# Page gathers that wait for score bursts, and cache copies moved into the second feed-forward block, in a two-layer hybrid decoder step

## The chip, the cores and the metric

One Trainium2 chip, one NeuronCore of it. The metric is the device time of one execution in microseconds (us), the median of several. A core has TensorE (PE; its weight loads are PEld), VectorE (DVE), ScalarE (ACT), GpSimd (POOL), SyncE (SP, which here only issues transfers), and 16 DMA engines that all queues share.

## What is computed

One inference step of a two-layer decoder for 256 prompt tokens and 8 samples of 8 tokens with 2048 past positions each, in float32. Each layer is a feed-forward block, token mixing, and a second feed-forward block:

```python
x += 0.5 * post1(SwiGLU_1(pre1(x)))
h  = pre_mix(x); proj = h @ w_in          # columns for branches A, B, C and gates
#   A: RWKV-7 time mixing;  B: dilated window attention;  C: latent attention
m = sum_b gate_b * (y_b @ w_branch_b);  x += post_mix(m @ w_out)
x += 0.5 * post2(SwiGLU_2(pre2(x)))
```

Branch C for a sample attends over 16 pages of a paged cache, found through a page table:

```python
ckv=cache_mla_ckv[l][page_table]          # 8 samples x 2048 rows x 256
s = (einsum('bqhc,blc->bhql', ql, ckv_all) + einsum('bqhr,blr->bhql', qr, krope_all)) * scale
return einsum('bhql,blc->bqhc', softmax(masked(s)), ckv_all)
```

Besides the result, the step returns the new states. Among them are the windows of keys and values of branch B for each sample: the old window without its first 8 rows, followed by the new ones. So 2040 of 2048 rows are copied from input to output, for 8 samples, keys and values, both layers.

## The kernel before

All engines run their own instruction streams, written out by hand, and meet on counting semaphores. `S[name]` counts steps, and `wait_ge(S[name], n)` waits until n of them are done.

**The samples' latent attention** (`ml_sample`, on TensorE, VectorE and ScalarE). For sample b, TensorE runs a burst of 144 matmuls of 32 rows by 64 columns on 256 keys (`scores`, which counts `ml_mm` at its end), then small pieces (`by_channel`, `own_tokens`), the value product of the sample before (`values(b - 1)`, 34 matmuls, counts `ml_pv`), and the transposes of the shares (`shares(b, r)`), the last of which takes the own tokens' share from VectorE. VectorE turns gathered keys into the layout that `scores` needs (`keys`: the low half of sample b+1 first in the round, before the maximum of sample b; the high half after it), takes the maximum over PSUM, and writes the own share (`own_share`). ScalarE takes the exponential.

**Page gathers** (GpSimd, from line 682). For each sample three indirect transfers of 2.25 MB together (one of the rotated keys, two of the latent rows, L698 and L701) go into one of four buffers. Before, those of samples 2 and 3 wait for the prompt's attention, those of samples 4 to 7 for `ml_pv` of b - 3, that is for the value product that last read the buffer. In time, this is just ahead of the burst of sample b - 2.

**Window copies** (GpSimd, `copied`, L674). 16 copies of 4080 KB, from DRAM to DRAM, in each layer, each waiting for the one before. `COPY_AT = (3, 11)`: three run from the input projection on, eight during the RWKV stage, and the last five right behind the last gather, that is during the last samples' attention and the output projection.

**Feed-forward weights** (SyncE, L646). A ring of three slots. A unit of the first half is 1 MB of gate and 1 MB of up weights (`f2 gu u`, 11 units), loaded when the unit three before it has been used; for unit 3 that is `ffn_gu` reaching 4, the end of unit 0. VectorE makes sums of quarters of unit u+1 during unit u (`weight_sums`, L2096 to L2102, a Strassen-like scheme), and TensorE waits for the second of these sums in unit u+1. The third branch's weights (`br c`) are loaded when `ml_pv` reaches 5.

The functions around the change, with the line numbers of the profile:

Of the kernel before, what the change touches and what calls it, by code (L numbers as in the profile page):

```python
# [141 lines left out]
GU0, SG0, TOK0 = {"f1": 0, "f2": 2}, {"f1": 0, "f2": 12}, {"f1": 0, "f2": 17}  # L142
# [137 lines left out]
def build(nc, io):  # L280
    SCB, SCC = DH ** -0.5, (DNOPE + DROPE) ** -0.5
    with ExitStack() as ctx:
# [3 lines left out]
        def sem(name):  # L286
            return ctx.enter_context(nc.semaphore(name))
# [33 lines left out]
        def cut(buf, at, a, b, rows=P):  # L321
# [85 lines left out]
        kr_at = [(big, 3072, big, 5120, big, 7168), (reg, 10720, reg, 12768, reg, 14816), (ring, 0, ring, 2048, ring, 4096),  # L407
                 (ring, 9088, h_flat, 0, h_flat, 2048)]
        KRc = [[cut(b0, at0, 8, KV_LORA), cut(b1, at1, 8, KV_LORA)] for b0, at0, b1, at1, _, _ in kr_at]
        KRr = [buf[:, at:at + 512] for _, _, _, _, buf, at in kr_at]  # L410
        QL = reg[:, 2016:15328].rearrange("p (c n) -> p c n", c=2)
        KTl = [cut(ring, 4608 + 2048 * i, 4, 512) for i in range(2)]
# [21 lines left out]
        S = {n: sem(n) for n in STEPS}  # L434
# [5 lines left out]
        units = weight_units(io)  # L440
        slot_of, before = weight_slots(units)
        uidx = {name: i for i, (name, _) in enumerate(units)}

        heads = [("f1", "gu", u) for u in range(HEAD)]
# [39 lines left out]
        def layer_begun(eng, l):  # L484
            eng.sem_inc(s_arrive, 1)
            eng.wait_ge(s_go, l + 1)
            eng.sem_inc(s_pad, 1)

        def lay(ap, l):
            return ap[bass.ds(l, 1)]  # L490
# [166 lines left out]
        @block.gpsimd  # L657
        def _(pool):
            for i in range(8):
                pool.dma_start(ptab[N_PAGES * i:N_PAGES * i + N_PAGES, :], io["page_table"].rearrange("b n -> n b"), allow_slow_non_contiguous=True).then_inc(s_copy, 16)  # L660
            pool.wait_ge(s_copy, TABLE)
            for l in range(DEPTH):
                layer_begun(pool, l)

                def copied(first, last):
                    for i in range(first, last):
                        if i:

                            pool.wait_ge(s_copy, l * (16 * 2 * NB) + TABLE + 16 * i)
                            pool.sem_inc(s_pad, 1)  # L670
                        b, n = i // 2, "kv"[i % 2]
                        src = lay(io["cache_swa_" + n], l)[:, b, TS:PAST].rearrange("a r n -> (a r n)")
                        dst = lay(io[f"o_swa_{n}_s"], l)[:, b, 0:PAST - TS].rearrange("a r n -> (a r n)")
                        pool.dma_start(dst.rearrange("(q n) -> q n", q=240),  # L674
                                       src.rearrange("(q n) -> q n", q=240)).then_inc(s_copy, 16)

                pool.wait_ge(S["pam"], 1)
                copied(0, COPY_AT[0])
                pool.wait_ge(S["streams"], 1)
                copied(COPY_AT[0], COPY_AT[1])  # L680
                pool.wait_ge(S["pages_ready"], 1)
                for b in range(NB):
                    if b == 0:
                        pool.wait_ge(S["sws_done"], NB)
                    elif b == 1:
                        pool.wait_ge(S["prompt_mm"], 2 * H + 16)
                        pool.wait_ge(S["ml_prep"], 1)
                    elif b in (2, 3):

                        pool.wait_ge(S["prompt_y"], 2 * H)  # L690
                        pool.wait_ge(S["ml_prep"], 1)
                        pool.wait_ge(S["pgm"], 24)
                    else:

                        pool.wait_ge(S["ml_pv"], b - 3)
                    rows_of = lambda i: bass.IndirectOffsetOnAxis(ap=pidx[:, i * NB + b:i * NB + b + 1], axis=0)
                    src = io["cache_mla_krope"].rearrange("l n (s r) c -> (l n s) (r c)", s=8)
                    pool.indirect_dma_start(out=KRr[b % 4], out_offset=None, in_=src, in_offset=rows_of(0)).then_inc(s_kr[b % 4], 16)  # L698
                    src = io["cache_mla_ckv"].rearrange("l n (s r) c -> (l n s) (r c)", s=16)
                    for half in range(2):  # L700
                        pool.indirect_dma_start(out=KRc[b % 4][half].rearrange("p n c -> p (n c)"), out_offset=None, in_=src, in_offset=rows_of(1 + half)).then_inc(s_kr[b % 4], 16)  # L701
                copied(COPY_AT[1], 2 * NB)
                pool.wait_ge(s_copy, l * (16 * 2 * NB) + TABLE + 16 * 2 * NB)

# [2133 lines left out]
```

## Time and profile before

| | |
|---|---|
| median of 3 runs | 2613.18 us (2611.27 to 2618.77) |
| profiled execution | 2636.64 us, its span 2634.8 us |
| granted TensorE clock, mean | 0.99 |
| TensorE busy | 2542.8 us (97%) |
| VectorE busy | 1314.5 us (50%) |
| ScalarE busy | 560.7 us (21%) |
| DMA moved | 505.66 MB, mean 192 GB/s |

The page gives one profiled execution on a time axis that starts at its span. "Idle before, releaser" tells how long an engine stood still ahead of an instruction and what ended that; "issue" means that nothing the profile shows did. PEclk is the clock granted to TensorE, 1.00 being 2.4 GHz and 0.50 1.2 GHz. The first layer ends near 1320 us; the second repeats its pattern some 1303 us later.

### The profile page before, as it was taken

Reading aid. Unit: us, or ns where it says so; the run is one execution under the profiler, and the core shown is the slowest. Engines: PE = TensorE matmul, PEld = TensorE weight load, DVE = VectorE, ACT = ScalarE, POOL = GpSimd, SP = SyncE. Lnnn points to the kernel's source line nnn. Section 1 sums busy time; section 2 is a strip of 40 time slices with the busy share of each in tenths; the row PEclk is TensorE's granted clock in tenths of the full one; section 3 lists DMA queues with packets and bytes.
Section 4 is the critical chain, followed back from the end, with each engine's and each line's share of the span. In section 5 each row is a group of like instructions: output and inputs, shape, how many; then the busy total and the mean of one; then the engine's idle time right before and its main releaser. Section 6 shows DMA issues by size and latency. Waiting matters only on the chain.

```text
span 2634.8 us, 52961 instructions
## 1 busy us (share of the span) xinstructions
PE 2542.8 (97%) x23108; PEld 2063.0 (78%) x23108; DVE 1314.5 (50%) x2847; ACT 560.7 (21%) x1249; POOL 67.4 (3%) x92
## 2 busy tenths in 40 slices
PE   7999999999999999999999999999989999999998
PEld 6999856655666667999999997566556666689998
DVE  4663553335543372665376535533455334627654
ACT  2110231133422221301021112311334222221010
POOL 0000000000000110000000000000000001100000
PEclk9999999999999899999999999999999998999999
DMA  6434679632962469544544456684439433794443
GB/s 228 145 114 143 225 241 335 225 122 117 383 262 71 157 214 373 162 132 118 144 146 131 120 175 248 226 321 177 173 134 395 181 120 137 272 333 147 131 111 86
DMA packets 260549, 505.66 MB, mean 192 GB/s; under 512 B 9760, under 2 KB 198560, under 8 KB 245216
## 3 DMA queue, kind: packets, MB, share of 16 engines
q1 hardware_dynamic: 251616, 330.83, 38.0%
q0 software_dynamic: 8704, 171.45, 17.6%
q8 instruction: 183, 3.00, 0.5%
q14 instruction: 46, 0.38, 0.0%
HBM read 491.95 MB, written 140.85 MB: 240 GB/s over the span
## 4 chain that ended last, share of the span: by engine, by line
PE 89%; DVE 5%; ACT 2%; DMA 2%; issue 1%; PEld 0%; SPq 0%; DVEq 0%
PE ps L716 84%; PE ps L719 6%; DMA big<-in_cache_swa_k_dram 1%; DMA ring<-in_f_wu_dram 1%; PEld ps L716 0%; ACT big L1841 0%; DVE reg L2009 0%; ACT reg L1841 0%; DVE ring L2507 0%; DVE x L2001 0%; DVE reg L2290 0%; SPq L580 0%; DVE reg L2584 0%; ACT reg L1712 0%; DVE ring L2522 0%
## 5 line engine op out<-in xcount | busy, mean ns | idle before, releaser
L716 PE MATMUL ps<-reg 128*128 128x160 f32 (+12 forms) x4584 | 513.2, 292 | 2.5 <-issue 1.6
L716 PEld LDWEIGHTS ps<-reg 128*128 128x128 f32 (+5 forms) x4584 | 453.7, 163 | 34.5 <-issue 25.1
L716 PE MATMUL ps<-h,ring 128*128 128x320 f32 (+2 forms) x1984 | 449.0, 378 | 17.4 <-DMA ring<-in_f_wu_dram 13.5
L716 PE MATMUL ps<-reg,ring 128*128 128x160 f32 (+1 forms) x3040 | 458.9, 306 | 0.0
L716 PEld LDWEIGHTS ps<-reg,ring 128*128 128x128 f32 x3040 | 426.1, 189 | 16.4 <-issue 6.2
L716 PEld LDWEIGHTS ps<-h,ring 128*128 128x128 f32 (+1 forms) x1984 | 323.0, 189 | 108.4 <-issue 28.5
L716 PE MATMUL ps<-ring,h 128*128 128x512 f32 (+3 forms) x896 | 246.6, 469 | 0.0
L716 PE MATMUL ps<-big,ring 128*128 128x160 f32 (+2 forms) x2016 | 214.6, 279 | 7.6 <-DVE big L2427 4.5
L716 PEld LDWEIGHTS ps<-big,ring 128*128 128x128 f32 (+2 forms) x2016 | 197.7, 168 | 28.2 <-issue 17.3
L716 PEld LDWEIGHTS ps<-ring,h 128*128 128x128 f32 (+1 forms) x896 | 103.1, 163 | 78.8 <-issue 62.9
L716 PE MATMUL ps<-big,reg 32*64 32x256 f32 (+8 forms) x2144 | 144.9, 363 | 3.3 <-issue 3.2
L716 PEld LDWEIGHTS ps<-big,reg 32*64 32x64 f32 (+4 forms) x2144 | 107.4, 139 | 30.9 <-issue 22.9
L719 PE MATMUL ps<-cst,big 128*128 128x128 f32 (+1 forms) x672 | 98.3, 283 | 18.4 <-ACT big L1841 7.3
L719 PEld LDWEIGHTS ps<-cst,big 128*128 128x128 f32 (+1 forms) x672 | 72.2, 140 | 38.9 <-ACT big L1841 12.4
L716 PE MATMUL ps<-ring,reg 32*64 32x256 f32 (+2 forms) x1312 | 90.3, 403 | 4.8 <-issue 3.4
L716 PE MATMUL ps<-ys,ring 128*128 128x320 f32 x256 | 79.0, 454 | 8.9 <-DVE reg L2555 8.9
L716 PE MATMUL ps<-ring 128*16 128x128 f32 (+3 forms) x1888 | 86.1, 261 | 0.0
L1687 ACT ACTIVATE reg<-ps 128x320 f32<-128x320 f32 x40 | 17.5, 439 | 316.8 <-PE ps L716 316.8
L719 PE MATMUL ps<-cst,reg 128*128 128x128 f32 (+3 forms) x436 | 73.5, 288 | 11.0 <-ACT ring L1895 6.0
L716 PEld LDWEIGHTS ps<-ring 128*16 128x16 f32 (+3 forms) x1888 | 69.8, 111 | 14.6 <-issue 13.6
L716 PEld LDWEIGHTS ps<-ring,reg 32*64 32x64 f32 (+1 forms) x1312 | 49.5, 140 | 38.7 <-issue 26.6
L719 PEld LDWEIGHTS ps<-cst,reg 128*128 128x128 f32 (+3 forms) x436 | 50.3, 143 | 33.4 <-issue 16.2
(320 smaller groups left out, 2642.3 us busy)
## 6 DMA issues: line engine op xcount, KB each, us to landing
out_o_swa_k_s_dram<-in_cache_swa_k_dram POOLq DMA_DIRECT2D x16, 4080.0 KB, 15.3
out_o_swa_v_s_dram<-in_cache_swa_v_dram POOLq DMA_DIRECT2D x16, 4080.0 KB, 16.5
ring<-in_w_in_dram SPq DMA_DIRECT2D x30, 2048.0 KB, 8.9
ring<-in_f_wd_dram SPq DMA_DIRECT2D x32, 1408.0 KB, 7.0
ring<-in_f_wg_dram SPq DMA_DIRECT2D x42, 1024.0 KB, 5.5
ring<-in_f_wu_dram SPq DMA_DIRECT2D x42, 1024.0 KB, 8.1
big<-in_cache_swa_k_dram SPq DMA_DIRECT2D x32, 1024.0 KB, 8.2
ring<-in_cache_swa_v_dram SPq DMA_DIRECT2D x32, 1024.0 KB, 7.2
```

The costliest lines, as they stand in the source:

```text
L716: return pe.matmul(out, lhsT, rhs, start=first, stop=last, skip_group_check=True)
L719: return pe.transpose(out, in_, ident[0:rows, 0:rows])
L1687: act.activation(GU[u % 2][:, :, 0, 0:HT], summed(X), ACT.Copy).then_inc(S["gu_act"], 1)
```

## The change

GpSimd gets three more waits. The gathers of samples 2 and 3 also wait for the first score burst (`ml_mm` 1), those of samples 4 to 7 for the burst of sample b - 2, counted from zero (`ml_mm` b - 1). The last five copies of the layer wait until unit 0 of the second feed-forward block is done (`ffn_gu` 4, the same point that releases the load of its unit 3). Nothing else is changed; in particular the transfers are the same.

```diff
                         pool.wait_ge(S["prompt_y"], 2 * H)
                         pool.wait_ge(S["ml_prep"], 1)
                         pool.wait_ge(S["pgm"], 24)
+                        pool.wait_ge(S["ml_mm"], 1)
                     else:
 
                         pool.wait_ge(S["ml_pv"], b - 3)
+                        pool.wait_ge(S["ml_mm"], b - 1)
                     rows_of = lambda i: bass.IndirectOffsetOnAxis(ap=pidx[:, i * NB + b:i * NB + b + 1], axis=0)
...
                         pool.indirect_dma_start(out=KRc[b % 4][half].rearrange("p n c -> p (n c)"), out_offset=None, in_=src, in_offset=rows_of(1 + half)).then_inc(s_kr[b % 4], 16)
+                pool.wait_ge(S["ffn_gu"], GU0["f2"] + 2)
                 copied(COPY_AT[1], 2 * NB)
```

## Rows read from the trace of the kernel before

**Rows 1.** The page, busy time, share of the span, instructions
```profile
PE 2542.8 (97%) x23108; PEld 2063.0 (78%) x23108; DVE 1314.5 (50%) x2847; ACT 560.7 (21%) x1249; POOL 67.4 (3%) x92
```

**Rows 2.** Windows over score bursts and both layers' loops; the last three: clock, DMA, GB/s
```profile
899.28:911.40 12.12, 10.70 (x148) 5.72 (x147) 0.31 (x2) 0.00 (x0) 5.37 (x6) 0.72 0.85 314
917.16:923.11 5.95, 5.95 (x146) 3.88 (x145) 5.18 (x11) 0.70 (x2) 0.00 (x0) 0.67 0.02 4
929.02:935.21 6.19, 5.37 (x146) 3.90 (x145) 2.91 (x8) 0.79 (x3) 1.95 (x3) 1.00 0.77 258
...
979.70:983.77 4.07, 4.07 (x145) 3.25 (x144) 2.56 (x8) 0.80 (x3) 0.00 (x0) 1.00 1.28 428
...
899.28:996.74 97.46, 88.93 (x1486) 59.63 (x1484) 60.50 (x139) 21.79 (x55) 17.75 (x20) 0.93 0.64 233
2202.47:2298.75 96.28, 89.72 (x1484) 59.68 (x1483) 60.49 (x139) 21.80 (x55) 17.71 (x20) 0.93 0.64 233
```

**Rows 3.** Timeline of TensorE: start, duration, what, idle before and its releaser
```profile
915.01 1.97 PE L719 MATMUL ps<-cst,reg 128*128 128x128 f32 x8 [3.01 <-ACT ring L1895]
...
932.38 0.53 PE L716 MATMUL ps<-ring,reg 32*64 32x256 f32 x6 [0.77 <-issue]
...
941.53 0.24 PE L719 MATMUL ps<-cst,ring 64*64 64x64 f32 x1
```

**Rows 4.** Timeline of GpSimd: gathers of samples 2 and 4, first and last of five copies
```profile
899.01 0.95 POOL L698 DMA_INDIRECT ring<-in_cache_mla_krope_dram,pidx  x1 [12.57 <-PE ps L716]
...
928.16 0.94 POOL L698 DMA_INDIRECT big<-in_cache_mla_krope_dram,pidx  x1 [21.98 <-PE ps L716]
...
969.64 0.55 POOL L674 DMA_DIRECT2D out_o_swa_v_s_dram<-in_cache_swa_v_dram  x1
...
1042.92 0.50 POOL L674 DMA_DIRECT2D out_o_swa_v_s_dram<-in_cache_swa_v_dram  x1 [16.85 <-DMA out_o_swa_k_s_dram<-in_cache_swa_k_dram]
```

**Rows 5.** Windows of 1 us at the ends of two gathers' data
```profile
914.00:915.00 1.00, 0.00 (x0) 0.00 (x0) 1.00 (x2) 0.96 (x4) 0.00 (x0) 0.61 0.08 33
...
937.00:938.00 1.00, 1.00 (x12) 0.68 (x10) 0.88 (x5) 0.72 (x1) 0.00 (x0) 1.00 0.14 57
```

**Rows 6.** Timeline of VectorE in the third sample's round: maximum, own share, key transposes
```profile
935.32 1.23 DVE L2705 TENSOR_REDUCE sml<-ps 128x1 f32<-128x1024 f32 x1 [3.18 <-PE ps L716]
...
940.71 0.15 DVE L2717 COPY ring<-ring 64x8 f32<-64x8 f32 x1
...
940.89 2.37 DVE L2650 STREAM_TRANSPOSE ring<-big 128x1024 f32<-128x1024 f32 x2
```

**Rows 7.** Timelines in the second feed-forward block: SyncE, VectorE (unit 3, 4), TensorE
```profile
1084.71 0.37 SPq L646 DMA_DIRECT2D ring<-in_f_wg_dram  x1
...
1109.38 1.22 DVE L2096 TENSOR_TENSOR reg<-ring 128x1024 f32<-128x1024 f32 x1
...
1124.59 1.22 DVE L2096 TENSOR_TENSOR reg<-ring 128x1024 f32<-128x1024 f32 x1
...
1117.12 2.34 PE L716 MATMUL ps<-reg 128*128 128x160 f32 x16
```

**Rows 8.** Time to landing, loads issued at 996.9, 1021.7, 2298.9, 2323.7, 1085.1
```profile
ring<-in_w_out_dram SPq DMA_DIRECT2D x1, 2048.0 KB, 28.6
...
ring<-in_f_wu_dram SPq DMA_DIRECT2D x1, 1024.0 KB, 38.1
...
ring<-in_w_out_dram SPq DMA_DIRECT2D x1, 2048.0 KB, 15.9
...
ring<-in_f_wu_dram SPq DMA_DIRECT2D x1, 1024.0 KB, 37.4
...
ring<-in_f_wu_dram SPq DMA_DIRECT2D x1, 1024.0 KB, 9.0
```

**Rows 9.** DMA queues from 1042.9 to 1060: packets, MB, share of 16 engines
```profile
q0 software_dynamic: 80, 4.18, 65.9%
q1 hardware_dynamic: 1805, 1.82, 33.5%
```

## The prediction

> **What bounds the kernel now.** I read the page first, then TensorE's waits, then the sample part of latent attention by windows, and last what the DMA engines do beside it. TensorE is busy for 97% of the span [rows 1], so only what stretches or idles TensorE counts. The place that the change touches is the loop over the eight samples, 97.5 us in the first layer and 96.3 us in the second [rows 2]. Each sample has one burst of 144 small score matmuls. With no gather in flight the seventh burst takes 4.07 us; the third takes 6.19 us and the first 12.12 us, both beside gathers; the second, with idle DMA, takes 5.95 us at a granted clock of 0.67 [rows 2]. The bursts of samples 4 to 6 are like the third (6.16 to 6.19 us). Inside the third, TensorE stands still for 0.77 us with "issue" as the only reason [rows 3]. These holes come 2 to 4 us after GpSimd starts issuing a gather [rows 4] and are over by about 1.2 us after its last issue, though the data flies on until 937. What starves is therefore the supply of instructions to a very dense burst, at the start of a gather, and not the data.
>
> **Part one: the gathers wait for the bursts.** The gather for sample b (4 to 7) now starts at the end of burst b-1 instead of at the end of the value product before it. It then runs beside the value product, whose matmuls are about a quarter as dense, and should be out of its starving phase before the next burst, 6.5 us later (the burst of the third sample ends at 935.2, the next begins at 941.7). In itself that is 6.17 - 4.07 = 2.1 us for each of four bursts. But the gather starts later, and a new wait may end last. Its flight is 9.3 us from first issue (928.2) to last data (about 937.5) [rows 4, 5]. Then VectorE turns the keys (2.37 us) and makes a divisor before it may take the next maximum, with some eight small instructions another 1.2 us: 3.6 us in all. From the maximum to the end of the own share 5.5 us pass (935.32 to 940.86) [rows 6], and TensorE needs that share at 941.53, 6.3 us after the burst's end at 935.2 [rows 3]; the slack is 0.8 us. So burst b+1 ends no earlier than 0.3 + 9.3 + 3.6 + 5.5 + 0.2 + 4.1 = 23.0 us after burst b-1, where two undisturbed periods would be 2 x 10.6 = 21.2 us and two of now are 25.3 us. Over bursts 4 to 8 this gives about 56.5 us against 61.5 us in the first layer (935.2 to 996.7), where copies also cost the last two samples some 1.5 us, and 59.9 us in the second.
>
> One collision is new. The load of the third branch's weights (2 MB) starts after the fifth value product; that comes 5 us into the flight of the last gather, where before the gather had landed. Two transfers share the engines for some 2.5 us, so I charge 2 us in each layer. Gains here: 3 us and 1.5 us.
>
> The first two bursts: the gathers for samples 2 and 3 (six issues in some 7 us from 899.0 on, data until about 914) [rows 4, 5] move from the first burst's start to its end. The first burst should then take 4.1 us, a gain of 8.1 us. The wait of 3.0 us for the exponential behind it stays [rows 3], and with it the fall of the clock to half. The second burst now meets the end of the six issues: I take the 3 us that it overlaps as nearly lost (some 15 of 144 matmuls, the density of the first burst at 904 to 907), and the rest partly at full clock, since the low clock now covers less of it. That comes to 7 us against 5.95 us. Keys for sample 2 are in by 13.8 us after the stretch's start, 3.6 us before the second maximum wants them: it comes at most 0.5 us late. The stretch up to the third burst's end goes from 35.9 to about 26.8 us, a gain of 9.1 us (9.5 us in the second layer). **Sum of part one: 12.1 + 11.0 = 23 us**, bounds 14 and 31 us: the low end has a half clock through the whole second burst (3 us a layer) and 0.4 us of holes in each value product; the high end has gathers that are fast enough for the undisturbed period.
>
> **Part two: the last five copies move.** They leave the end of the attention and the output projection, where TensorE never waits for weights, and start when the first unit of the second feed-forward block is done, at 1084.7, together with the load of unit 3 [rows 7]. GpSimd's queue has nothing behind them until the next layer, so the wait for f2 itself costs nothing. The loads are what counts. That block takes one unit of 2.1 MB per 15.2 us. Unit 3's sums begin at 1109.38 and unit 4's at 1124.59 [rows 7], with loads issued at 1084.7 and 1097.75. TensorE takes the second sum at 1117.12, 3.5 us of VectorE work after the landing, so unit 3 may land up to 28.9 us after 1084.7, and the following ones up to 44.1, 59.3 and 74.5 us. Without copies such a load lands in 9.0 us [rows 8].
>
> Beside copies it doesn't. The five copies stand 17 to 21 us apart (969.6 to 1042.9) [rows 4]. In the stretch of the last of them, with weights waiting all through it, the weights' queue (q1) moved 1.82 MB in 1805 packets in 17.1 us, the copy's (q0) 4.18 MB in 80 [rows 9]; the block wants 2.36 MB in that time. Counted from the copy issued at 990.8, the first 2.1 MB asked for after it landed at 34.6 us (996.9 + 28.6) and the third 2.1 MB at 69.0 us (1021.7 + 38.1); in the second layer the first landed at 21.3 us (2298.9 + 15.9, copy at 2293.5), the third at 67.6 us [rows 8]. Against the limits of 28.9 and 59.3 us the third unit is late by 8.3 to 9.7 us in both layers, and the fourth, one copy period of 17.2 us on, by some 10 to 13. Lateness here isn't added up: each wait moves the later limits. So a layer loses the largest, **11.5 us, 23 us in both**, bounds 0 and 27 us. Zero is possible, since copies and loads start together and the average rate (0.12 MB per us over the two last copies) falls short by only 2.3 us a unit, which the slack of 9.7 us would just cover if landings weren't lumpy. I take the landings, since they are the same thing measured twice. A fall of the clock in such a wait costs up to 3 us in each layer and is in the upper bound.
>
> The trace's rows show why: weights come in lumps between copies. The Trainium skill, "DMA: Bandwidth & Descriptors", section "Queues, rings and completion order", says that a DMA engine alternates between the queues that have work, a whole packet at a time. That speaks against this change, since a copy's packets are long and the weights' rows short, and the trace agrees. By the page the loss would be that of the landings, by the average rate next to nothing.
>
> **The sum.** The profiled execution took 2636.6 us (its span 2634.8), 0.9% over the median of 2613.2 us; both terms are differences in microseconds and carry over. 2613.2 - 23 + 23 = **2613 us**. The gain of the samples is given back in the feed-forward block. For this likeliest case alone the range is 2604 to 2622 us.
>
> **The rivals.** (1) The copies are hidden in the feed-forward block: part one is kept, 2613 - 23 = 2590 us, 2582 to 2600 with its bounds. For it: the average rate, and a slack of two units; the second layer's first load fitted between two copies (21.3 us). Against it: both third loads. (2) Slower: the weights of the second feed-forward block, starved by copies, are late by the full 13.5 us with the clock falling in the waits, 2 x 15 = +30 us, while the sample loop gives only 14 us: 2629 us. It decides from the point where the loss of a layer exceeds 11.5 us. For it: two idle times of 3 us are each followed by half clock in the sample loop. (3) The holes aren't the gather's: the bursts keep their length wherever the gather stands, part one gives nothing and the gathers only come later, 2613 + 23 = 2636 us. Against it: the seventh burst, 4.07 us, in both layers. The Trainium skill, "Runtime: NRT & Kernel Launch", section "Instruction fetch mechanics", calls the crossing of an instruction block "mostly hidden"; by that rule part one would give nothing but the clock. The holes of 0.77 us speak against it.
>
> **Chances.** Forecast 0.52, (1) 0.28, (2) 0.14, (3) 0.06. Some 0.3% (8 us) is what a measurement of this kernel can tell from no change. Faster: (1) and 0.05 of the forecast's edge, 0.33; slower: (2), (3) and 0.02, 0.22; the same: 0.45. The range takes in most of (1) and of (2): 2588 to 2630 us.
>
> **What would show it.** First burst near 4.1 us, third to sixth near 4.1 us without issue holes, the period alternating between 10.6 and 12.4 us: part one. VectorE waiting on a gather's landing ahead of its key transposes: the 9.3 us are the bound. In the second feed-forward block: VectorE and TensorE waiting for weight landings of units 3 to 6, landings of 20 to 38 us instead of 9, and a block longer by some 11 us. If no such wait is there, part two is wrong and rival (1) holds. If the holes appear in the value products instead, part one only moved them.

## The result, and the profile after

The changed kernel took 2650.1 us (median of 4 runs, 2632.8 to 2654.6) against 2613.9 us before (4 runs, 2611.3 to 2618.8): a ratio of 1.013, interval 1.010 to 1.0159. The kernel got 36 us slower. The forecast was 2613 us in a range of 2588 to 2630, so the measured time lies 37 us above the forecast and 20 us above the range. The ratios in this document are given with their 95% interval as they were recorded; they are not the quotients of the two medians and lie up to 0.13% away from them, so differences of 0.1% are not read.

The profile's page of the kernel after, as [rows 1]: busy time, then the chain of work that ended last by engine, then the group of matmuls that waits most for weights.

```profile
PE 2535.9 (96%) x23108; PEld 2063.9 (78%) x23108; DVE 1313.9 (50%) x2847; ACT 559.0 (21%) x1249; POOL 67.4 (3%) x92
...
PE 85%; DVE 5%; DMA 4%; ACT 2%; issue 2%; PEld 0%; SPq 0%; POOL 0%; DVEq 0%; POOLq 0%
...
L719 PE MATMUL ps<-reg,ring 128*128 128x160 f32 (+1 forms) x3040 | 460.7, 306 | 11.4 <-DMA ring<-in_f_wu_dram 11.4
```

TensorE is busy for 7 us less than in [rows 1], and yet the profiled span is longer, 2652.8 us against 2634.8: what came are waits. Windows over the first six score bursts and the two loops, as [rows 2] (PE busy, PEld, DVE, ACT, POOL, then granted clock, DMA share, GB/s):

```profile
901.96:906.09 4.13, 4.13 (x148) 3.75 (x146) 0.31 (x2) 0.00 (x0) 0.00 (x0) 1.00 0.01 4
911.05:916.76 5.71, 5.71 (x145) 3.81 (x144) 2.77 (x3) 0.70 (x2) 2.53 (x3) 0.70 1.00 374
927.25:933.39 6.14, 6.14 (x145) 4.00 (x144) 2.98 (x8) 0.70 (x2) 0.00 (x0) 0.65 0.02 7
939.89:943.96 4.07, 4.07 (x146) 3.24 (x145) 0.00 (x0) 0.79 (x3) 0.00 (x0) 1.00 0.81 328
953.78:957.86 4.08, 4.08 (x146) 3.25 (x145) 3.07 (x7) 0.70 (x2) 0.00 (x0) 1.00 0.02 6
964.35:970.92 6.57, 4.71 (x146) 3.38 (x145) 2.15 (x2) 0.79 (x3) 0.00 (x0) 1.00 0.51 197
901.96:996.37 94.41, 80.97 (x1485) 57.09 (x1483) 60.09 (x139) 21.41 (x55) 16.95 (x18) 0.93 0.49 174
2219.10:2313.21 94.11, 80.95 (x1486) 56.99 (x1484) 60.36 (x139) 21.43 (x55) 16.94 (x18) 0.91 0.48 175
```

The first burst is whole, 4.13 us, as forecast. But the loops are only 3.1 and 2.2 us shorter than in [rows 2], not 12 and 11 us. (That pair turns out to be of two kinds of execution; the like for like comparison stands further down.) The reader sees where it went in VectorE's timeline, with GpSimd's of the gathers that it waits for:

```profile
907.01 0.95 POOL L700 DMA_INDIRECT ring<-in_cache_mla_krope_dram,pidx  x1 [17.90 <-PE ps L719]
...
934.33 0.95 POOL L700 DMA_INDIRECT big<-in_cache_mla_krope_dram,pidx  x1 [20.14 <-PE ps L719]
...
918.12 2.37 DVE L2653 STREAM_TRANSPOSE ring<-ring 128x1024 f32<-128x1024 f32 x2 [4.30 <-DMA ring<-in_cache_mla_ckv_dram,pidx]
...
921.62 1.21 DVE L2708 TENSOR_REDUCE sml<-ps 128x1 f32<-128x1024 f32 x1
...
944.53 2.37 DVE L2653 STREAM_TRANSPOSE ring<-big 128x1024 f32<-128x1024 f32 x2 [5.40 <-issue]
```

and in TensorE's:

```profile
925.11 1.97 PE L722 MATMUL ps<-cst,reg 128*128 128x128 f32 x8 [3.56 <-ACT ring L1898]
...
951.52 1.09 PE L722 MATMUL ps<-cst,reg 128*128 128x128 f32 x8 [1.27 <-ACT ring L1898]
953.61 0.24 PE L722 MATMUL ps<-cst,ring 64*64 64x64 f32 x1 [1.00 <-DVE ring L2720]
...
970.33 0.65 PE L719 MATMUL ps<-big 32*64 32x256 f32 x6 [1.86 <-issue]
...
972.04 5.36 PE L719 MATMUL ps<-big,reg 128*64 128x256 f32 x32
...
1170.56 4.04 PE L719 MATMUL ps<-reg,ring 128*128 128x160 f32 x16 [10.18 <-DMA ring<-in_f_wu_dram]
```

VectorE stands ahead of the key transposes until a gather has landed: 11.1 us after its first issue for sample 2 (907.01 to 918.12), 10.2 us for sample 4 (934.33 to 944.53). For sample 2 the view names the transfer. For sample 4 it says "issue", and the reading rests on the DMA share, which is 0.28 from 943 to 944 and 0.00 from 944 to 945. The maximum, due at 916.9 when the second burst ends, is taken at 921.62; TensorE idles 3.56 us, the clock falls, and the third burst runs for 6.14 us at a granted clock of 0.65. The last line is in the second feed-forward block: one unit's weights are 10 us late, and their issue on SyncE's queue itself took 23 us, where it takes 0.58 us in the trace of before:

```profile
1143.44 23.43 SPq L646 DMA_DIRECT2D ring<-in_f_wu_dram  x1
```

Two profiles 18 us apart don't explain medians 36 us apart, and the profiled execution of before was 23 us above the median of the timed runs of the same kernel. What lay in that 23 us is what the experiments had to find.

### The profile page after: what moved, and what is told of

It is laid out like the page before. It is cut to its first block, busy times and chain, and to the rows that moved or that the text cites. A ratio compares the mean times of both kernels' runs of the same rounds, so it can differ in the third digit from the quotient of the medians.

```text
span 2652.8 us, 52973 instructions
## 1 busy us (share of the span) xinstructions
PE 2535.9 (96%) x23108; PEld 2063.9 (78%) x23108; DVE 1313.9 (50%) x2847; ACT 559.0 (21%) x1249; POOL 67.4 (3%) x92
## 4 chain that ended last, share of the span: by engine, by line
PE 85%; DVE 5%; DMA 4%; ACT 2%; issue 2%; PEld 0%; SPq 0%; POOL 0%; DVEq 0%; POOLq 0%
PE ps L719 79%; PE ps L722 6%; DMA ring<-in_f_wu_dram 3%; DMA ring<-in_cache_mla_ckv_dram,pidx 1%; ACT big L1844 1%; PEld ps L719 0%; ACT reg L1844 0%; DVE reg L2012 0%; DMA reg<-in_cache_mla_ckv_dram,pidx 0%; DMA h<-in_cache_mla_ckv_dram,pidx 0%; DVE ring L2510 0%; DVE ring L2653 0%; DVE x L2004 0%; DVE reg L2293 0%; DVE big L2653 0%
## 5 line engine op out<-in xcount | busy, mean ns | idle before, releaser
L719 PE MATMUL ps<-reg,ring 128*128 128x160 f32 (+1 forms) x3040 | 460.7, 306 | 11.4 <-DMA ring<-in_f_wu_dram 11.4
L719 PEld LDWEIGHTS ps<-ring,h 128*128 128x128 f32 (+1 forms) x896 | 103.8, 165 | 80.1 <-issue 64.3
L719 PE MATMUL ps<-big,reg 32*64 32x256 f32 (+8 forms) x2144 | 136.2, 359 | 0.2 <-issue 0.2
L1690 ACT ACTIVATE reg<-ps 128x320 f32<-128x320 f32 x40 | 17.5, 437 | 308.6 <-PE ps L719 308.6
L719 PE MATMUL ps<-ring,reg 32*64 32x256 f32 (+2 forms) x1312 | 78.3, 433 | 0.0
L1693 ACT ACTIVATE ys<-reg 128x640 f32<-128x640 f32 x40 | 29.5, 737 | 209.1 <-DVE reg L2243 209.1
## 6 DMA issues: line engine op xcount, KB each, us to landing
out_o_swa_v_s_dram<-in_cache_swa_v_dram POOLq DMA_DIRECT2D x16, 4080.0 KB, 16.8
```

The lines of the kernel that those rows point to most:

```text
L719: return pe.matmul(out, lhsT, rhs, start=first, stop=last, skip_group_check=True)
L1690: act.activation(GU[u % 2][:, :, 0, 0:HT], summed(X), ACT.Copy).then_inc(S["gu_act"], 1)
L1693: act.activation(SG[u % 2], GU[u % 2][:, 0], ACT.Sigmoid).then_inc(S["ffn_sg"], 1)
```

## The experiments

The runs were made in five groups. All ratios are to the kernel before, timed in the same group on the same chip.

**First group: the parts alone.** Both gather waits, copies at their old place; the copies alone; and the waits of samples 4 to 7 alone. Each leaves the other added lines out (cut):

```diff
 # gathers_only, both lines; late_gathers_only, the second alone
+                        pool.wait_ge(S["ml_mm"], 1)
+                        pool.wait_ge(S["ml_mm"], b - 1)
 # copies_only
+                pool.wait_ge(S["ffn_gu"], GU0["f2"] + 2)
```

> Part one alone: the gathers of samples 2 to 7 wait for the bursts, the last five copies stay behind the last gather. Theory A (the loss sits in the second feed-forward block, the sample loop gains a little): 2609 us, 0.1 to 0.4% under before, the stretch of a layer's eight bursts some 94 us instead of 97. Theory B (the gathers' new waits cost more than the bursts gain): over before by 0.5% or more, 2627 us and up, with waits of VectorE on gather landings ahead of its key transposes.

Measured: 2642.4 us against 2643.5, ratio 0.9992 (0.9976 to 1.0008). That is neither of the two theories and not a gain of 23 us: no difference shows.

> Only the gathers of samples 4 to 7 wait for a burst; those of samples 2 and 3 start as before, and the copies stay. Against part one whole it tells what the wait of the first two costs: theory A' (moving them idles TensorE ahead of the third burst and keeps its clock low, so they are worth only the 8 us of the first burst less some 8 us): within 3 us of part one whole. Theory B': they carry the gain, and this kernel is 5 us or more slower than part one whole.

Measured: 2650.7 us, 1.0023 (1.0007 to 1.004): this half costs 6 to 7 us. An issue hole (idle time that the profile ends with "issue" alone) of 2.68 us stands in its last burst.

> Part two alone: the gathers start where they did, the last five copies start after unit 0 of the second feed-forward block. Theory A: the whole loss is here, 2640 to 2650 us (+1.0 to 1.4%), with one or more waits of TensorE on weights landing in the second feed-forward block of each layer. Theory B: within 0.4% of before.

Measured: 2648.4 us, 1.0022 (1.0003 to 1.0041): 5 us lost, not 23.

The fourth kernel is the changed one with the last five copies of a layer each cut into two DMAs of alternate 2 KB rows (only the main lines are shown; the semaphore counts change with them):

```diff
+                        if i >= COPY_AT[1]:
+                            src = lay(io["cache_swa_" + n], l)[:, b, TS:PAST].rearrange("a (r e) n -> (a r) e n", e=2)
+                            dst = lay(io[f"o_swa_{n}_s"], l)[:, b, 0:PAST - TS].rearrange("a (r e) n -> (a r) e n", e=2)
+                            for e in range(2):
+                                pool.dma_start(dst[:, e], src[:, e]).then_inc(s_copy, 16)
+                            continue
```

> The changed kernel, with each of the last five copies of a layer split into its even and its odd rows of 2 KB, so that its packets are about as short as the weights'. Theory of the packets (a DMA engine takes turns between queues by packet, so long copy packets hold up the weights): the waits for weights in the second feed-forward block vanish, 10 us or more faster than the changed kernel, 2610 to 2640 us. Rival (the engines' total rate is the bound, 0.38 MB per us for both): waits and time as in the changed kernel, 2650 us.

Measured: 2630.6 us, 0.9955 (0.9938 to 0.9973), the first version below before. The copies' DMA queue and the weight loads from 1080 to 1170 us, first in the changed kernel (`changed_once_more`, below) and then in this one (packets, MB, share of 16 engines; for the loads KB each and median us to landing):

```profile
q0 software_dynamic: 398, 20.89, 62.1%
...
ring<-in_f_wg_dram SPq DMA_DIRECT2D x6, 1024.0 KB, 24.0
ring<-in_f_wu_dram SPq DMA_DIRECT2D x6, 1024.0 KB, 25.5
```

```profile
q0 software_dynamic: 4332, 17.15, 56.0%
...
ring<-in_f_wg_dram SPq DMA_DIRECT2D x7, 1024.0 KB, 12.1
ring<-in_f_wu_dram SPq DMA_DIRECT2D x6, 1024.0 KB, 16.8
```

The copies go in eleven times as many packets for 18% fewer bytes in that stretch, and the weights land in 12.1 and 16.8 us instead of 24.0 and 25.5; TensorE waits for no weight in that block, in either layer. The chip doesn't explain it: `copies_only`, timed beside this kernel, has 23.7 and 25.4 us. So the length of the copies' packets made the weights late. In exchange the copies themselves move more slowly when cut: 17.15 MB against 20.89 MB in the 90 us, while the weights' queue moves 12.58 MB against 9.22. The Trainium skill, "DMA: Bandwidth & Descriptors", section "Queues, rings and completion order", has an engine alternate between queues by whole packets; this pair of rows agrees.

**Second group: again, and the copies taken apart.**

> The changed kernel on the same footing as the partial ones. By the sum of the two parts measured alone (-1 us and +5 us) it is 2 to 6 us over before, ratio 1.000 to 1.003. If the two parts hinder each other, or if the first measurement holds wherever it is run, it is 1.3% (30 us or more) over before.

Measured: 2642.4 us against 2645.4, ratio 1.0001 (0.9981 to 1.0021). The 1.3% was gone, with the kernel unaltered. In its trace TensorE waits 2.6 us for weights in the first layer's block where the trace of after waits 10.2.

The next two have the gathers of before; the copies are cut as above, and stand in the second feed-forward block or at their old place. The third leaves the last five copies of each layer out (two outputs stay incomplete).

> The gathers as before; the last five copies in the second feed-forward block, split into rows of 2 KB. If short packets alone bring the gain: 2630 us, 13 us under before. If it needs the gathers' new waits too: within 3 us of before less the 5 us that the long-packet copies cost there, about 2640 us.

Measured: 2638.5 us, 0.9978 (0.9959 to 0.9998).

> The kernel before with nothing changed but the packets of the last five copies of a layer (rows of 2 KB). If long packets of the copies also hold up the fetch of TensorE's instructions in the last bursts: 2 to 8 us under before, without issue holes in the seventh and eighth burst. If only the place counts: as before.

Measured: 2642.3 us, 0.9992 (0.9972 to 1.0012): inconclusive.

> The kernel before without the last five copies of each layer (that part of the window copies is left out). It tells what copies at the old place cost: by the trace of before some 1.5 us of issue holes in the first layer and 0.2 us in the second, so 0 to 4 us under before. If it is 10 us or more under before, the copies cost more at their old place than the trace's holes show, and moving them has that much to win.

Measured: 2636.0 us, 0.9969 (0.9952 to 0.9986). These copies cost about 8 to 9 us where they were (4 to 13 us by the interval), in stages for which the prediction had charged them 1.5 us.

**Third group: is before itself the same each time?** Two kernels unaltered, the changed one without the last copies, and the changed one with all sixteen copies cut.

```diff
 # late_gathers_no_last_copies, on the changed kernel
-                pool.wait_ge(S["ffn_gu"], GU0["f2"] + 2)
-                copied(COPY_AT[1], 2 * NB)
 # all_copies_in_2kb_rows, on copies_in_2kb_rows
-                        if i >= COPY_AT[1]:
+                        if True:
```

> The kernel before, unaltered, as a run of its own. It tells what the ruler is worth. The first comparison had before at 2613.9 us and the changed kernel at 2650.1 us; on two later chips before stood at 2643.5 and 2645.4 us and the changed kernel at 2642.4 us. Theory: the absolute time of before depends on the chip, and the two are equal on each of them; then this run has a ratio of 1.000 +- 0.002, and its absolute time is again in 2640 to 2648 us. Rival: before has executions near 2613 us that the changed kernel lacks; then some of these twelve are under 2625 us.

Measured: 2613.0 us against 2613.9, ratio 0.9997 (0.9984 to 1.0011). Within the group before repeats itself, and the level is not the 2644 us of the first two groups.

> The changed kernel, unaltered, beside before on a further call. Theory (the changes cancel): ratio 0.998 to 1.003, some 2642 us if before is at 2644 us. Rival (the first comparison, 1.3% slower, is what the change does): ratio above 1.008, 2665 us.

Measured: 2647.1 us, 1.0126 (1.0109 to 1.0143). The 1.3% was back. So the changed kernel took 2642 to 2650 us in all three comparisons, and before is what moves, between 2613 and 2644. Windows over the first three bursts and over both loops in the trace of `before_again`, to be laid beside [rows 2]:

```profile
899.44:903.58 4.14, 4.14 (x148) 3.75 (x146) 0.31 (x2) 0.00 (x0) 3.23 (x4) 1.00 0.54 135
908.54:914.30 5.76, 5.76 (x146) 4.29 (x145) 5.62 (x9) 0.70 (x2) 0.00 (x0) 0.70 0.93 382
920.21:924.28 4.07, 4.07 (x146) 3.24 (x145) 3.10 (x8) 0.79 (x3) 1.97 (x3) 1.00 0.66 197
...
899.44:979.55 80.11, 75.25 (x1486) 55.21 (x1484) 60.35 (x139) 21.78 (x55) 17.78 (x20) 0.98 0.74 271
2192.71:2273.80 81.09, 76.86 (x1486) 55.47 (x1484) 60.45 (x139) 21.79 (x55) 17.75 (x20) 0.96 0.74 272
```

The same program, the same gather issued 0.3 us ahead of the first burst (899.17), and the burst takes 4.14 us, not 12.12. The third takes 4.07 us beside its gather (DMA share 0.66). The loops take 80.1 and 81.1 us against 97.5 and 96.3: 32.5 us in both. One microsecond of each burst, in the profile that I had and in `before_again`:

```profile
901.00:902.00 1.00, 0.93 (x9) 0.44 (x12) 0.00 (x0) 0.00 (x0) 0.69 (x2) 1.00 0.76 229
```

```profile
901.00:902.00 1.00, 1.00 (x49) 1.00 (x41) 0.00 (x0) 0.00 (x0) 0.69 (x2) 1.00 0.66 217
```

The gather moves as much (229 and 217 GB/s) at the same full clock, and TensorE starts 9 matmuls or 49. A gather beside a burst is not enough to stretch it. I call the two kinds of execution stretched and whole.

> The changed kernel with the last five copies of each layer left out (two outputs stay unwritten for the last samples). The same left out of the kernel before gave 2636.0 us against 2645.4 us, a ratio of 0.9969. So this run against that one is the worth of the late gathers with no copies about. Theory (the gathers' holes are traded against waits for their landing and half-clock bursts): within 3 us of 2636 us at a before of 2645 us, ratio 0.995 to 0.998. Rival (my first sum: part one is worth 23 us): 2613 us, ratio 0.988.

Measured: 2637.1 us, 1.0087 (1.007 to 1.0104) against a whole before (four runs). The late gathers alone cost over 23 us there; the copies in the feed-forward block add 10 us (2647.1 - 2637.1).

> The changed kernel with all sixteen copies of a layer, not only the last five, split into two DMAs of 2 KB rows each. With the last five split it took 2630.6 us against 2643.5 us, a ratio of 0.9955. Theory (long packets make weight loads late only where the load has little slack, which is the second feed-forward block): the first eleven copies lie beside projections and prompts that don't wait for weights, so nothing more is gained; ratio 0.994 to 0.997. Rival (long packets cost wherever copies run): another 5 us or more, ratio under 0.993. Doubled issues on GpSimd could also cost: then above 0.998.

Measured: 2626.5 us, 1.0052 (1.0035 to 1.007), 20.6 us below the changed kernel of its group. That is more than leaving the last copies out gives, so the rival holds: the first eleven copies' long packets cost too, over 10 us, and where exactly isn't settled (no single wait that went stands out in their stages).

**Fourth group: a trace of a stretched before beside its time, and the halves.** `only_samples_2_and_3_wait` has of the change only the first added wait; the two others are kernels of above.

> The kernel before, unaltered, with a trace. Theory (stretched bursts are the whole difference between before at 2613 us and before at 2644 us): if its median is above 2635 us, its first score burst takes some 12 us and the bursts of samples 2 and 4 to 6 some 6.2 us, 11 to 13 us a layer; if it is under 2620 us, all bursts but the second take some 4.1 us. Rival (the level differs for another reason, all over the span): a slow one with whole bursts, or a fast one with stretched bursts.

Measured: 2640.2 us against 2644.8 (0.9988, 0.9972 to 1.0003). Windows over the fourth burst and over both loops:

```profile
944.48:950.74 6.26, 5.74 (x146) 3.78 (x145) 2.59 (x8) 0.80 (x3) 1.98 (x3) 1.00 0.79 267
901.76:998.95 97.19, 88.83 (x1486) 59.86 (x1484) 60.52 (x139) 21.79 (x55) 17.78 (x20) 0.93 0.64 233
2209.53:2306.10 96.57, 88.28 (x1486) 59.80 (x1484) 60.52 (x139) 21.79 (x55) 17.79 (x20) 0.93 0.64 234
```

Stretched, with a time at the upper level: its loops are 32.6 us longer than those of `before_again` (97.2 + 96.6 against 80.1 + 81.1), its profiled execution 32.3 us (2643.95 against 2611.63). In this pair the stretched loops are the whole difference of level. The profile that the prediction was made from differs from `before_again` by 32.5 us of loops too, but by only 25.0 us in all: between the two loops it is 7.4 us shorter, in stages that are the same program. Single executions vary by that much elsewhere.

> The second part alone: the last five copies in the second feed-forward block, gathers as before. On a chip where before took 2643.5 us it cost 4.8 us (ratio 1.0022). Theory: the loss is one of weight landings and has nothing to do with the bursts, so it is the same on any chip: 3 to 9 us more than before, ratio 1.001 to 1.0035. Rival (the second part costs more where the bursts are whole): ratio above 1.005.

Measured: 2642.9 us, 0.9988 (0.9975 to 1.0001). With the 1.0022 of the first group: between -2 and +5 us, for a part that I had at +23.

> Half of the first part: the gathers of samples 2 and 3 wait for the first score burst, those of samples 4 to 7 start as before, copies as before. Waiting of samples 4 to 7 alone gave 1.0023, both waits 0.9992, on a chip with stretched bursts. Theory: there this half is the good one, since it mends the 12 us burst and costs one landing wait: ratio 0.994 to 0.998. On a chip with whole bursts it only brings the landing wait and the half-clock burst behind it, some 6 us a layer: ratio 1.003 to 1.006. Rival (the waits of the first part are what costs everywhere): above 1.000 on either.

Measured: 2629.6 us, 0.9956 (0.9931 to 0.9982), on a stretched before; five runs only, from 2619.3 to 2641.1. This is the good half, as expected, though VectorE waits 4.71 us for sample 2's gather in its trace.

> Gathers as before, last five copies in the second feed-forward block and split into two DMAs of 2 KB rows. It gave 0.9978 on a chip where before took 2645.4 us. Theory: short packets take the loss of the second part away and keep the copies from the end of the attention, on any chip: ratio 0.996 to 0.9995. Rival: on a chip where before takes 2613 us nothing is to be had from the copies: ratio 1.000 to 1.003.

Measured: 2636.7 us, 0.9965 (0.995 to 0.998).

**Fifth group: the landing wait, priced.** Old gathers but for sample 3, or samples 2 and 3; last copies cut and in the second feed-forward block.

```diff
 # samples_2_and_3_wait_2kb: without the condition
+                        if b == 3:
+                            pool.wait_ge(S["ml_mm"], 1)
```

> Only the gathers of samples 2 and 3 wait for the first score burst; last five copies in the second feed-forward block as 2 KB rows. The two halves gave 0.9956 and 0.9965 to 0.9978 alone. Theory (their gains lie in different stages and add): 0.992 to 0.995 where before takes some 2644 us (2623 to 2631 us); where before takes 2614 us, the landing wait of sample 2 and the half-clock third burst cost 5 us a layer and the copies give 4 to 8: 1.000 to 1.004. Rival: they don't add, 0.996 or more, or 1.006 or more on a chip with whole bursts.

> As the other kernel of this call, but only sample 3's gather waits for the first burst; sample 2's starts beside it as in the kernel before. Theory (the landing of sample 2's gather is what this half costs): no idle time for it ahead of the third burst's round, on any chip. Where bursts are stretched, three issues remain beside the first burst, which then takes 6 to 8 us instead of 12, the third burst has full clock, and the total is that of the other kernel within 3 us. Where bursts are whole: 3 to 10 us below the other kernel, at or just below before, ratio 0.997 to 1.000. Rival (any gather beside the first burst, ahead of the exponential's wait, costs the whole stretch): first burst 10 us or more on a chip with stretched bursts, 8 us or more above the other kernel.

The record gives the same chip number for this group and the first one, and before now took 2616.0 us, not 2643.5. So the expectations above, which put whole and stretched down to the chip, are wrong in that: one chip showed both, and in the fifth group the fourth and fifth bursts, beside unchanged gathers, took 4.07 us in both traces. Measured: 2618.9 us, 1.0012 (0.9998 to 1.0026), with both samples waiting; 2607.6 us, 0.9967 (0.9953 to 0.9982), with sample 3 alone. Loops of the one and of the other:

```profile
897.54:980.98 83.44, 76.83 (x1486) 55.14 (x1484) 60.45 (x139) 21.67 (x55) 16.94 (x18) 0.96 0.55 197
2193.84:2279.10 85.26, 79.46 (x1486) 56.42 (x1484) 60.53 (x139) 21.66 (x55) 16.93 (x18) 0.92 0.54 193
```

```profile
906.89:985.90 79.01, 75.39 (x1486) 54.41 (x1484) 60.33 (x139) 21.77 (x55) 16.64 (x18) 0.98 0.57 208
2200.15:2278.88 78.73, 75.46 (x1486) 54.93 (x1484) 60.33 (x139) 21.78 (x55) 16.65 (x18) 0.98 0.58 209
```

11.0 us of loop, 11.3 us of median, and all of the 11.0 lies ahead of the third burst's end (29.5 against 24.8 us from the loop's start in the first layer, 32.0 against 25.7 in the second). The two kernels differ only in the wait of sample 2's gather, so its late landing is the price of moving it: in the first layer a 3.26 us wait of TensorE, the next 2.14 us at a granted clock of 0.50 and a third burst of 4.54 us, in the second layer a third burst of 7.66 us at 0.62. In the kernel where sample 3 alone waits the third bursts took 4.07 and 4.89 us. (The two profiled executions are only 0.2 us apart, since that of the second kernel spent 9.4 us more ahead of the loop, where the kernels are the same; it is the slowest of its six runs.) The second version is the only one that beat a whole before, by 0.3% (0.9967, 0.9953 to 0.9982); it was not run against a stretched one.

## Why the prediction was wrong

**The step that failed** is the sentence that the profiled execution lay 0.9% over the median and "both terms are differences in microseconds and carry over". They were not of the same thing. The profile was of a stretched execution (its loops of 97.5 and 96.3 us are like the 97.2 and 96.6 of `before_on_another_chip`); that the median of 2613.2 us was of whole ones is read from its level, that of `before_again`. The 23.4 us between them were not noise around a common kernel; part one's gain of 23 us was the mending of what those runs did not have. From the whole kernel's 80.1 and 81.1 us the changed loops of 93.9 us are 26.6 us longer:

```profile
901.10:995.03 93.93, 80.80 (x1486) 57.91 (x1484) 60.40 (x139) 21.42 (x55) 16.92 (x18) 0.93 0.48 175
2212.04:2305.95 93.91, 81.72 (x1486) 57.25 (x1484) 60.27 (x139) 21.47 (x55) 16.95 (x18) 0.91 0.48 175
```

Those two rows are of `changed_once_more`. Its waits for weights in the second feed-forward block are 3.8 us in the first layer (2.2 + 1.6 below) and 3.5 in the second; 26.6 + 7.3 = 33.9 us of the 36.5 us between its profiled execution and that of `before_again`. The remaining 2.6 us are not traced; stages that the change doesn't touch vary by more than that.

```profile
PE ps L719 <- DVE reg L2103: 2.2, 2, 1.2
PE ps L719 <- DMA ring<-in_f_wu_dram: 1.6, 1, 1.6
```

**Part one against a stretched before** is a term of the sum that was mis-sized. The fair pair for it is a changed kernel in a group where before is stretched. Both loops of `changed_again`, and its second burst:

```profile
903.21:994.12 90.91, 78.88 (x1486) 56.03 (x1484) 60.27 (x139) 21.44 (x55) 17.00 (x18) 0.96 0.50 181
2207.77:2299.30 91.53, 80.62 (x1486) 57.25 (x1484) 60.45 (x139) 21.44 (x55) 16.98 (x18) 0.93 0.49 180
912.32:919.24 6.92, 6.58 (x145) 4.17 (x144) 2.99 (x4) 0.70 (x2) 2.53 (x3) 0.78 0.98 376
```

Against [rows 2] that is 6.5 and 4.8 us of loop, 11.3 us in both, where 12.1 and 11.0 were forecast; the low bound was 14. The first burst took 4.14 us (forecast 4.1) and the second 6.92 (forecast 7). The gather of sample 2, with the three issues of sample 3 behind it, took 10.75 us from its first issue to the key transposes, not 9.3. TensorE idled 1.93 and 0.67 us ahead of the third burst, whose end came 28.8 us after the stretch's start, not 26.8. From there to the eighth burst's end it took 62.1 us, where 56.5 us and 2 us for a collision were forecast and 61.5 us stand in the trace of before: this is the larger part of the miss.

The trace of after, of the group with a whole before, shows the same steps at a higher price. Its second burst took 5.71 us and was done at 14.8 us from the stretch's start; the keys, forecast "in by 13.8 us" with the maximum "at most 0.5 us late", were in at 16.2 us (918.12 - 901.96), and the maximum came 4.7 us late. The idle time of 3.56 us dropped the clock on the third burst (+2.1 us), which the forecast had charged nowhere; its end came 31.4 us after the stretch's start. From the third burst's end to the fifth's, forecast at 23.0 us, 24.5 us passed (933.39 to 957.86): 0.94 us from the burst's end to the issue instead of 0.3, 10.2 us to the transposes instead of 9.3. From the fourth's end to the sixth's it was 27.0 us and from the fifth's to the seventh's 25.3 us, with new starvation, as the forecast's last sentence allowed: a hole of 1.86 us in the sixth burst and a value product of 5.36 us for 3.67.

The value product starts just behind the gather issued at 971.78; the value product at 946.01, as close behind one, takes its 3.67 us, so why this one is long isn't settled. The hole is tied to a place in the program and not to that gather. Nine of the traces have an issue hole at this very place in the first layer, with six matmuls of the burst left, among them `changed_again`, `samples_2_and_3_wait_2kb` and `only_sample_3_waits_2kb`, and none of the three traces of before has one:

```profile
968.71 0.65 PE L719 MATMUL ps<-big 32*64 32x256 f32 x6 [1.67 <-issue]
959.02 0.66 PE L727 MATMUL ps<-big 32*64 32x256 f32 x6 [0.26 <-issue]
```

In all nine a packet of the instruction queue (q8 in the profile) starts 0.4 to 2.2 us ahead of the hole. That the hole waits for it is likely and not shown.

**Part two**: mechanism right, size wrong. Landings went from 9.0 us [rows 8] to some 24 us, inside the 20 to 38 forecast, and VectorE and TensorE waited for weights as forecast, though later in the block (from 1138 to 1181 us). But the waits cost TensorE 7.3 us in `changed_once_more`, 10.2 us for one unit in the profile of after, and -2 to +5 us net in the two runs of the copies alone, not 23. One thing was left out: the copies had a price at the old place (8 to 9 us in `without_last_copies`), which moving them gives back. One was over-sized: the term took the latest of two landings in a row for the whole block, where the average rate would just have covered it. The slack of 9.7 us in that argument is worked out nowhere; by the prediction's own numbers it is 28.9 us less 17.5 us for a unit at the average rate, 11.4 us, and five units at 2.3 us use up just that. The measured waits lie between the two ways of counting.

**The sum.** Nothing gained and little lost is what stretched comparisons show (0.9992, 1.0001), and the forecast of "the same" was right there by luck, for two wrong terms that cancel. For whole executions rival 3 came nearest in number (2636 us), and it had right that part one gives nothing and the gathers only come later. But it charged nothing for their coming later, which is 26.6 us of loop, and 23 us for the weights, which is 7.3; and its claim that the bursts keep their length wherever the gather stands is wrong for stretched executions (12.1 us against 4.1). It was given 0.06 on the strength of the seventh burst; that burst shows that no gather means no stretch, and says nothing on whether a gather must bring one.

**What starves in a stretched burst.** The prediction called it the supply of instructions. The profile lists the transfers of instructions as queues q8 and q14. Between the start of the first burst and the next packet of either queue, in the trace of before and in `before_again`:

```profile
899.28:906.69 7.41, 6.12 (x81) 2.89 (x80) 0.31 (x2) 0.00 (x0) 5.37 (x6) 0.82 0.74 251
```

```profile
899.44:902.24 2.80, 2.80 (x108) 2.80 (x114) 0.31 (x2) 0.00 (x0) 2.19 (x3) 1.00 0.48 117
```

The same program had started 108 matmuls before its next instruction packet when whole, and only 81 when stretched. So what TensorE was slow to start had been fetched already, and the 0.77 us hole at 903.86 is over 2 us before the packet begins. As far as the profile lists them, late instruction packets are not what stretches the first burst; what does, no trace tells. The Trainium skill, "Runtime: NRT & Kernel Launch", section "Instruction fetch mechanics", calls the crossing of an instruction block "mostly hidden". The stretched first burst doesn't speak against it; the holes of 0.26 to 1.97 us in the sixth burst may.

## What to carry to other kernels

Before terms read from one profile are set against a median, ask whether that execution is one of those timed: a gap between them that is as large as a term of the sum is itself the first thing to explain. Making a transfer wait for a moment when it can do no harm starts it late; write down its landing, from first issue to the consumer's start with the neighbours' issues in the queue, beside the consumer's due time. Where long copies run beside loads that have little slack, cut the copies' packets short: in the second feed-forward block that turned -2 to +5 us for moving them into -7 to -8 us, while the cut alone, at the old place, showed nothing clear (0.9992, 0.9972 to 1.0012).

## What was not expected

One program has two levels, 2613 to 2616 us and 2640 to 2645 us. Over the 13 to 35 runs of before in a group they don't mix (no run from 2622.9 to 2631.6 us), and they differ between groups, on one chip too if the chip number in the record is the same chip. Most of the difference stands in how many matmuls TensorE starts beside the opening microseconds of a gather, 9 or 49 in the one shown, with the gather's bytes and the clock the same. The changed kernel shows the two kinds as well, but in its second burst, which runs beside the last issues: 6.92 us in `changed_again` against 5.71 us in the trace of after. There it doesn't pay in time, since VectorE waits for the gather either way: 2642.4 us in the group of the one kind, 2647.1 and 2650.1 us in the two of the other. What sets the kind, the placement of something in memory or otherwise, no run here tells; it stays open.
